# Sums over the partitions as two fp32r products of a split sum, the latents' squares added on GpSimd, and small moves on TensorE and VectorE

## The reference

```
h = concatenate([meta, x])                                # 272 x 1024
h = h + ssd_mixer(rms_norm(h, ln_mix[0]))                 # 8 groups of 256 channels, 4 heads each
h = h + square(relu(rms_norm(h, ln_mlp[0]) @ w_up)) @ w_down
h = h + mla_mixer(rms_norm(h, ln_mix[1]))                 # 16 heads, latents of 384 (q) and 256 (kv)
h = h + square(relu(rms_norm(h, ln_mlp[1]) @ w_up)) @ w_down
x = h[16:]                                                # 256 x 1024
x = x + (sigmoid(ga)*(na(q, k, v) @ w_a) + sigmoid(gb)*(cb*conv3(cc*ch) @ w_b)) @ w_o
x = x + square(relu(rms_norm(x) @ w_mlp_in)) @ w_mlp_out

# in ssd_mixer, for each of the 8 groups:
g = y * silu(z);  g = g * rsqrt(mean(g*g over the group's 256 channels) + eps)
# rms_norm: x * rsqrt(mean(x*x over the channels) + eps) * gain
```

## Time and profile before

| | |
|---|---|
| median of 3 executions | 1103.89 us (1103.84 to 1104.99) |
| profiled execution | 1103.82 us |
| its span | 1102.1 us |
| granted TensorE clock | 1.00 over the span |
| TensorE, VectorE, ScalarE, GpSimd busy | 99%, 70%, 59%, 15% |

### The profile page before, as it was taken

How to read it: one execution, slowest core, us unless ns; L and a number is a source line. 1 busy time by engine, 2 the same in 40 slices (tenths; PEclk the granted TensorE clock), 3 DMA queues, 4 the chain that set the end, 5 groups by cost and what they waited for, 6 DMA issues and landing times.

```text
span 1102.1 us, 24005 instructions
## 1 busy us (share of the span) xinstructions
PE 1094.4 (99%) x8963; PEld 1066.9 (97%) x8963; DVE 771.8 (70%) x1153; ACT 653.9 (59%) x1075; POOL 170.6 (15%) x152
## 2 busy tenths in 40 slices
PE   9999999999999999999999999999999999999998
PEld 8999999999999999988899999999999999999998
DVE  8999999778665555688676665558787687666543
ACT  7899999555554343577565554446555755554331
POOL 0445444326000000111010000000003201000000
PEclk9999999999999999999999999999999999999999
DMA  7454444575454555332265555555444555555552
GB/s 267 181 186 163 169 157 173 153 249 172 171 171 172 179 178 175 136 135 98 83 218 177 189 189 181 180 193 173 153 154 154 185 181 190 180 182 191 187 180 90
DMA packets 53226, 189.96 MB, mean 172 GB/s; under 512 B 5920, under 2 KB 7200, under 8 KB 53168
## 3 DMA queue, kind: packets, MB, share of 16 engines
q1 hardware_dynamic: 51408, 182.59, 48.4%
q0 software_dynamic: 1760, 6.59, 2.1%
HBM read 188.07 MB, written 1.08 MB: 172 GB/s over the span
## 4 chain that ended last, share of the span: by engine, by line
PE 85%; DVE 10%; ACT 2%; issue 2%; DMA 1%; POOL 0%; SPq 0%; DVEq 0%; ACTq 0%
PE lin L462 27%; PE lin L464 26%; PE lin L463 26%; DVE w_lo L1430 3%; DMA w_raw<-w 1%; PE ps L561 1%; DVE s_m L1836 1%; DVE x_lo L1440 1%; DVE p_t L1854 1%; ACT w_hi L948 0%; ACT pr L1351 0%; DVE s_m L1918 0%; PE ps L540 0%; DVE p_t L1941 0%; DVE q_ss L1779 0%
## 5 line engine op out<-in xcount | busy, mean ns | idle before, releaser
L1430 DVE TENSOR_TENSOR w_lo<-w_raw,w_hi 128x1024 fp32r<-128x1024 f32 (+3 forms) x318 | 392.6, 1237 | 237.6 <-ACT w_hi L948 236.6
L948 ACT ACTIVATE w_hi<-w_raw 128x1024 fp32r<-128x1024 f32 (+2 forms) x342 | 352.0, 1034 | 230.9 <-PE lin L464 222.0
L462 PE MATMUL lin<-x_hi,w_hi 128*128 128x256 f32 (+1 forms) x1504 | 432.1, 287 | 0.4 <-DVE x_lo L1440 0.4
L464 PE MATMUL lin<-x_hi,w_lo 128*128 128x256 f32 (+1 forms) x1504 | 428.3, 285 | 0.0
L463 PE MATMUL lin<-x_lo,w_hi 128*128 128x256 f32 (+1 forms) x1504 | 427.3, 284 | 0.0
L462 PEld LDWEIGHTS lin<-x_hi,w_hi 128*128 128x128 f32 x1504 | 283.6, 189 | 2.2 <-issue 0.8
L464 PEld LDWEIGHTS lin<-x_hi,w_lo 128*128 128x128 f32 x1504 | 283.8, 189 | 0.0
L463 PEld LDWEIGHTS lin<-x_lo,w_hi 128*128 128x128 f32 x1504 | 283.0, 188 | 0.6
L464 PE MATMUL lin<-hid_hi,w_lo 128*128 128x256 f32 (+1 forms) x768 | 218.2, 284 | 0.0
L463 PE MATMUL lin<-hid_lo,w_hi 128*128 128x256 f32 (+1 forms) x768 | 217.9, 284 | 0.0
L462 PE MATMUL lin<-hid_hi,w_hi 128*128 128x256 f32 (+1 forms) x768 | 217.4, 283 | 0.0
(11 more groups left out here) (301 smaller groups left out, 1505.5 us busy)
## 6 DMA issues: line engine op xcount, KB each, us to landing
w_raw<-w SPq DMA_DIRECT2D x342, 512.0 KB, 3.3
acs_bc<-acs_dram POOLq DMA_DIRECT2D x8, 544.0 KB, 5.9
bias_mask<-rpb POOLq DMA_DIRECT2D x4, 512.0 KB, 10.9
h<-h SPq DMA_DIRECT2D x4, 272.0 KB, 3.7
out<-h SPq DMA_DIRECT2D x8, 128.0 KB, 3.3
cst<-const SPq DMA_DIRECT2D x1, 808.0 KB, 7.1
vecs<-vec SPq DMA_DIRECT2D x1, 131.5 KB, 2.1
w_raw<-w SPq DMA_DIRECT2D x1, 128.0 KB, 4.7
```

Of the source, the lines that this page charges most:

```text
L462: mm3(o, wh, xh, start=first and i == 0, stop=False)
L464: ins = mm3(o, wl, xh, start=False, stop=last and i == kts - 1)
L948: a(w_hi[pg.slot][:, 0:n], w_raw[pg.slot][:, 0:n], ACT.Copy).then_inc(w_hi_done, pages)
L1430: tt(w_lo[pg.slot][:, 0:n], w_raw[pg.slot][:, 0:n], w_hi[pg.slot][:, 0:n].bitcast(F32), ALU.subtract)\
```

## The change

1. `group_stat`, eight times, and `norm_stat` for norms 1, 3 and 5: the fp32 product of ones with the sum becomes two fp32r products, of ones_r with the rounded sum and with the rest. GpSimd makes the rounded sum (the same addition with an fp32r output) and the rest (a subtraction that waits for both), so three operations a group in place of one, and two more a norm. ones_r is made by ScalarE in its first slot.
2. GpSimd adds kv's two tiles of squares into one and two of q's three (`add_latents`); the kv sum is three products in place of six, the q sum four in place of six.
3. `mout_part(0, ...)`: four k-tiles at t = 16 between scores(13) and p_transposes(10), in place of five at t = 17; t = 21 takes three in place of two.
4. VectorE at the start: w_lo of page 0 ahead of the last two g_lo.
5. VectorE in the second block: yb_lo from the end of i = 11 and 12 to i = 12 and 13, behind the copy of the transposed probabilities. Its operands are unchanged.

The buffers (ones_r, hs_hi, hs_lo, ys_hi, ys_lo, all fp32r) and the semaphores' declarations are left out of the diff.

```diff
@@ -485,6 +491,12 @@
             def norm_stat(norm):
                 n = width(norm)
+                if norm % 2:
+                    pe.wait_ge(hsplit_done, norm // 2 + 1)
+                    nc.tensor.matmul(ps7[:, 0:n], ones_r[:, :], hs_hi[:, 0:n], start=True, stop=False)
+                    nc.tensor.matmul(ps7[:, 0:n], ones_r[:, :], hs_lo[:, 0:n], start=False, stop=True)\
+                        .then_inc(stat_done, 1)
+                    return
                 pe.wait_ge(hsum_done, (KD - 1) * norm)
                 nc.tensor.matmul(ps7[:, 0:n], ones, h_sq[:, 0, 0:n], start=True, stop=True).then_inc(stat_done, 1)
...
@@ -545,7 +557,9 @@
             def group_stat(g):
                 pe.wait_ge(ysum_done, (g + 1).value)
                 pe.wait_ge(cbm_done, (g + 2).value) if g.base < 7 else None
-                nc.tensor.matmul(ps5[:, 0:T], ones, y_sum[:, :], start=True, stop=True).then_inc(gstat_done, 1)
+                pe.wait_ge(ones_r_done, 1)
+                nc.tensor.matmul(ps5[:, 0:T], ones_r[:, :], ys_hi[:, :], start=True, stop=False)
+                nc.tensor.matmul(ps5[:, 0:T], ones_r[:, :], ys_lo[:, :], start=False, stop=True).then_inc(gstat_done, 1)
             def y_products(g):
                 pe.wait_ge(xtok_done, (g + 1).value)
...
@@ -652,11 +666,9 @@
             lin_chunk(At(C_MIN), At(K_MIN), T, 2)
             norm_stat(2)
             lin_chunk(At(C_MIN + 1), At(K_MIN + 1), T)
-            pe.wait_ge(latsq_done, 1)
+            pe.wait_ge(latsum_done, 1)
             for b, t0 in enumerate(MLA_BLOCKS):
-                for i in range(2):
-                    ins = nc.tensor.matmul(ps5[:, b:b + 1], lat_sq[:, i, t0:t0 + P], ones[:, 0:1],
-                                           start=i == 0, stop=i == 1)
+                ins = nc.tensor.matmul(ps5[:, b:b + 1], lat_sq[:, 0, t0:t0 + P], ones[:, 0:1], start=True, stop=True)
             ins.then_inc(lstat_done, 1)
             lin_chunk(At(C_MIN + 2), At(K_MIN + 2), T)
...
@@ -666,12 +678,12 @@
             ins.then_inc(kpeT_done, 1)
             def q_stat():
-                pe.wait_ge(latsq_done, 3)
+                pe.wait_ge(latsum_done, 2)
                 pe.wait_ge(rln_done, 3)
                 for b, t0 in enumerate(MLA_BLOCKS[1:]):
-                    for i in range(3):
+                    for i in range(2):
                         ins = nc.tensor.matmul(ps7[:, b:b + 1], lat_sq[:, 3 + i, t0:t0 + P], ones[:, 0:1],
-                                               start=i == 0, stop=i == 2)
+                                               start=i == 0, stop=i == 1)
                 ins.then_inc(lstat_done, 1)
             def in_tokens(o, pg, kts, kt0, t0, n):
...
@@ -808,14 +820,14 @@
                     q_stat()
                 if 18 <= t < 21:
                     mout_part(t - 17, 5 if t < 19 else 3, 0)
-                if t == 17:
-                    mout_part(0, 5, 0)
                 if t >= 6 and t % 2:
                     p_transposes(t - 6)
                 if 1 <= t < 16 and t % 2:
                     turn_keys(t // 2)
                 if 3 <= t < 19:
                     scores(t - 3)
+                if t == 16:
+                    mout_part(0, 4, 0)
                 if t >= 6 and not t % 2:
                     p_transposes(t - 6)
                 if 2 <= t <= 16 and not t % 2:
...
@@ -823,7 +835,7 @@
                 if t in (19, 20):
                     mout_part(t - 17, 2, 3)
                 if t == 21:
-                    mout_part(0, 2, 5)
+                    mout_part(0, 3, 4)
                     mout_part(1, 2, 5)
                 if t >= 7 and t % 2:
                     values((t - 7) // 2)
...
@@ -1115,6 +1127,8 @@
                 hi((c + 3).page(0))
                 conv0(s, 1)
                 hi((c + 3).page(1))
+                act.wait_ge(const_in, 16)
+                a(ones_r[:, :], ones, ACT.Copy).then_inc(ones_r_done, 1)
                 hi((c + 4).page(0))
                 hi((c + 4).page(1))
                 for pair in range(2):
...
@@ -1475,10 +1489,10 @@
                 raw_lo(kt)
             square_raw(6)
             square_raw(7)
+            lo(Page(0), DT_PAGE)
+            dve.sem_inc(w_lo_done[1], 1)
             raw_lo(6)
             raw_lo(7)
-            lo(Page(0), DT_PAGE)
-            dve.sem_inc(w_lo_done[1], 1)
             lo(Page(2))
             dve.wait_ge(r_done, 1)
             r32 = slice(0, 32)
...
@@ -1939,6 +1953,11 @@
                     if i >= 10:
                         dve.wait_ge(pv2_done, 2 * ((i - 8) // 2))
                     nc.vector.tensor_copy(p_t2[i % 2][:, :], ps7[:, :]).then_inc(pt2_done, 1)
+                if i in (12, 13):
+                    j = i - 12
+                    dve.wait_ge(ybh_done, j + 1)
+                    tt(yb_lo[:, 2 * j:2 * j + 2, :], yb[:, 2 * j:2 * j + 2, :],
+                       yb_hi[:, 2 * j:2 * j + 2, :].bitcast(F32), ALU.subtract).then_inc(ybl_done, 1)
                 if i in (11, 12):
                     j = i - 11
                     dve.wait_ge(drained[(k + (-1)).parity], (k + (-1)).half + 1)
...
@@ -2005,13 +2024,6 @@
                             ALU.mult, ALU.add).then_inc(cv2_step, 1)
                 if 6 <= i < 14:
                     weigh2(i - 6)
-                if i in (11, 12):
-                    j = i - 11
-                    dve.wait_ge(ybh_done, j + 1)
-                    dve.wait_ge(yb_done, j + 1)
-                    tt(yb_lo[:, 2 * j:2 * j + 2, :], yb[:, 2 * j:2 * j + 2, :],
-                       yb_hi[:, 2 * j:2 * j + 2, :].bitcast(F32), ALU.subtract).then_inc(ybl_done, 1)
-
             for b in range(4):
                 c = At(C_BR + b)
...
@@ -2057,7 +2069,14 @@
                     pool.wait_ge(hsq_done, KD * norm + kt + 1)
                     if kt > 1:
                         pool.wait_ge(hsum_done, (KD - 1) * (norm - 1) + kt - 1)
+                    if norm % 2 and kt == KD - 1:
+                        tt(hs_hi[:, 0:n], h_sq[:, 0, 0:n], h_sq[:, kt, 0:n], ALU.add).then_inc(hs_hi_done, 1)
+                        pool.wait_ge(hs_hi_done, norm // 2 + 1)
                     tt(h_sq[:, 0, 0:n], h_sq[:, 0, 0:n], h_sq[:, kt, 0:n], ALU.add).then_inc(hsum_done, 1)
+                if norm % 2:
+                    pool.wait_ge(hsum_done, (KD - 1) * norm)
+                    tt(hs_lo[:, 0:n], h_sq[:, 0, 0:n], hs_hi[:, 0:n].bitcast(F32), ALU.subtract)\
+                        .then_inc(hsplit_done, 1)
             def lo(pg, n=PAGE):
...
@@ -2085,7 +2104,10 @@
                     lo((c + 2).page(1))
                 if has_stat:
                     pool.wait_ge(ysq_done, (gs + 1).value)
-                    tt(y_sum[:, :], h_sq[:, 0, :], h_sq[:, 1, :], ALU.add).then_inc(ysum_done, 1)
+                    tt(y_sum[:, :], h_sq[:, 0, :], h_sq[:, 1, :], ALU.add).then_inc(ysum_step, 1)
+                    tt(ys_hi[:, :], h_sq[:, 0, :], h_sq[:, 1, :], ALU.add).then_inc(ysum_step, 1)
+                    pool.wait_ge(ysum_step, (gs + 1).times(2).value)
+                    tt(ys_lo[:, :], y_sum[:, :], ys_hi[:, :].bitcast(F32), ALU.subtract).then_inc(ysum_done, 1)
                 if has_lin:
                     lo((c + 3).page(1))
                     if has_rows:
...
@@ -2130,6 +2152,12 @@
             for e in range(2):
                 tt(rope_q[:, :, e, :], angles[:, 1:3, :], over(cst[:, N_QGR:N_QGR + 64], 2), ALU.mult)\
                     .then_inc(rope_done, 1)
+
+            def add_latents(to, count):
+                pool.wait_ge(latsq_done, count)
+                tt(lat_sq[:, to, :], lat_sq[:, to, :], lat_sq[:, to + 1, :], ALU.add).then_inc(latsum_done, 1)
+
+            add_latents(0, 1)
             pool.wait_ge(kpe_step, 2)
             tt(kpe_sum[:, :, :], kpe_rot[:, :, 0:32], kpe_rot[:, :, 32:64], ALU.add).then_inc(kpefin_done, 1)
             pool.wait_ge(kpefin_done, 1)
...
@@ -2137,6 +2165,7 @@
             for e in range(2):
                 tt(kpe_fin[:, :, e, :], kpe_sum[:, :, :], kv_rms[:, :].unsqueeze(2).broadcast_to([P, 3, 32]), ALU.mult)\
                     .then_inc(kpefin_done, 1)
+            add_latents(4, 3)
             pool.wait_ge(kpefin_done, 3)
             pool.wait_ge(rope_done, 3)
             q_turn = rope_q[:, :, :, :].rearrange("p b h d -> p (b h) d")
```

More of the change, by code:

```diff
@@ L177, in build @@
         eps_t = sb("eps_t", [P, 4])
+        ones_r = sb("ones_r", [P, P], F32R)
+        hs_hi, hs_lo = [sb(f"hs_{n}", [P, T], F32R) for n in ("hi", "lo")]
         ssd = ExitStack()
@@ L208, in build @@
         y_sum = sb("y_sum", [P, T], F32, ssd)
+        ys_hi, ys_lo = [sb(f"ys_{n}", [P, T], F32R, ssd) for n in ("hi", "lo")]
         g_ln = sb("g_ln", [P, T], F32, ssd)
@@ L344, in build @@
         hsq_dve = sem("hsq_dve")
+        ones_r_done, hs_hi_done, hsplit_done = sem("ones_r_done"), sem("hs_hi_done"), sem("hsplit_done")
+        ysum_step = sem("ysum_step")
         rln_done, r_done = sem("rln_done"), sem("r_done")
@@ L367, in build @@
```

(1 more changed line is left out.)

## The result

The changed kernel takes 1125.34 us in the median of four executions (1124.41 to 1127.09), against 1104.15 (1103.84 to 1104.99) before: 1.019 times as long, 95% interval 1.018 to 1.021. It is slower by 21 us, where 1104.1 and no change were forecast. The profiled execution took 1124.67 us, its span is 1123.0, 20.9 more than before.

A forecast was written before the change was run, and what follows sets the result against it. TensorE, busy 99% of the span, was taken as the bound. Terms -2.2 - 0.6 + 0 + 0 + 3.1 - 0.3 + 0.8 - 0.5 = +0.3 gave 1104.1 us, 8-in-10 range 1100.5 to 1106.8.

The forecast's parts named there:

- The group sums' product: State-space part: two fp32r products in place of one fp32 product on TensorE save 0.20 us a group, eight 1.6.
- the norms: Three MLP norms: the same replacement of the fp32 product saves 0.2 + 2 x 0.19 = 0.58 us.
- the kv latents: Latents' squares: six of twelve one-column records on TensorE go, 0.105 each, -0.63 us.
- The queries' sum: Four records go, but TensorE's transposes wait for q_n, whose chain does not move: 0 taken, bound -0.42 us.
- the price of the turns in the steady slots: GpSimd's added operations each wait for one VectorE operation; ys_lo is ready before TensorE's 115.63: 0, bound +3.0 us.
- Rival (c): Steady slots: VectorE is the bound and a page comes late, up to 0.5 us a slot, 1107.1; chance 0.13.
- The tail: End of the state-space part: TensorE waits for ys_lo, +2.4 at group 6, +0.7 at group 7; +3.1 us, range +1.2 to +4.1.
- The start: TensorE's 0.33 idle at the dt products goes as w_lo comes earlier: -0.3 us, range 0 to -0.5.
- The projection's first tile: Near 524, moved products fill TensorE's waits but values(5) comes 0.45 later: +0.8 us, other bound -1.2.
- yb_lo: TensorE's 0.66 wait at 833.79 for a copy behind this operation shrinks: -0.5 us, range -0.2 to -0.65.

The follow-up runs named there:

- experiment 4: Changed kernel with the third x_tok (16 partitions) moved on VectorE from ahead of the first mm to between the two mm: 1106.48 us (1.0018).
- e5_no_start: Changed kernel with the group sums' change undone and the order at the start as before too: 1102.72 us (0.9987 of the kernel before).
- the first probe: VectorE and GpSimd alone, none of the reference computed; GpSimd released at 22 moments around a run of VectorE operations on 128 partitions: nothing over 1.66 us.
- the second, with a narrow operation ahead: VectorE and GpSimd alone, the slot's piece around ys_lo at 12 moments: with 16 partitions in the third x_tok 4.5 to 4.7 us at some, with 128 always 0.76.

## Why the prediction was wrong

- **The group sums' product, the norms, the kv latents** were right: a slot of 22.00 against 22.20; -0.21 at norm 1; -0.68 for -0.63. The queries' sum, forecast at 0 with a bound of -0.42, gave -0.3: the attention part takes 101.90 with it alone and 102.21 before.
- **The step that failed** is the price of the turns in the steady slots, GpSimd held off by "its neighbour's" length: "ys_hi follows until about 113.4, ys_lo until 114.3, at worst (each behind an operation of 0.9) 115.4". The worst case had each GpSimd operation behind one of VectorE's, as in every row of before. ys_lo was kept out by four. In the steady slots I took 0, bound +3.0, and it was +18.8: 3.2 us at the first sum and 2.7 at each of five more (24.69 for 22.00), with 3.1 of slower clock behind two of them, less 1.0 that the products save. Nothing of before shows such a case, because there no GpSimd operation starts between the narrow x_tok and the run; the bound was made from rows that had met only the easy case. What could be read in the same trace is the run itself, which the prediction did not lay beside its own times. Of VectorE, before:

```profile
113.67 2.01 DVE L1571 TENSOR_TENSOR mm<-ee,cbm 128x864 f32<-128x864 f32 x2
115.61 0.71 DVE L1547 TENSOR_TENSOR xs_s<-cv,sg 128x544 f32<-128x544 f32 x1
116.24 1.21 DVE L1430 TENSOR_TENSOR w_lo<-w_raw,w_hi 128x1024 fp32r<-128x1024 f32 x1
```

With ys_hi until 113.4, ys_lo would start some 0.3 ahead of this run, and a bound by the whole of it is 3.8.
- **Rival (c)** had the right sign for the wrong reason: VectorE was busy for a smaller share of the slots, and TensorE waited in them for ys_lo and for no page.
- **The tail** was mis-sized by phase: +1.1 net of what the products save there, for a forecast of +2.5 so counted (3.1 less three times 0.2). In the changed kernel everything comes at other moments there, group 6 does not wait, and group 7 waits 1.43. In the kernel of experiment 4, where the tail is reached as before, it costs +2.4, close to the forecast's. The range's lower end of 1.2 held group 6 alone; with the 0.65 of group 7 it is 1.8.
- **The start**: -0.3 forecast, range 0 to -0.5; +2.15 in the profiled execution. In the medians it is about +0.9 (1103.62 against 1102.72), from intervals that overlap. The sum took TensorE's row alone and had no term for the clamp and w_lo meeting. The explanation in the expectation of e5_no_start, that the earlier w_lo gets ahead of the clamp, does not hold: the clamp starts first, and at the same distance both outcomes are on record. Held clamps were seen with the new order only, in four of seven traces against none of six with the old; whether the order brings them is open.
- **The projection's first tile**: +0.8 forecast, +0.74 by the traces with and without it. **yb_lo**: -0.5 forecast; the wait at 833.79 is gone, and the second block with norm 5 is 0.72 shorter, 0.53 without the norm.

The terms that failed, the steady slots, the tail and the start, are all about GpSimd and VectorE meeting; the others were within 0.3. The Trainium skill ("SBUF — State Buffer", SBUF: two separate sides) says that whichever of the two starts first gets the shared pair of ports for its instruction. In the first probe, all on 128 partitions, the runs agree, down to 0.02 us. In the second, with a narrow operation ahead, they do not: ys_lo starts 0.20 ahead of mm and takes 4.59 for 0.76. Nor do they at the start, where the clamp begins 0.29 ahead of w_lo and is held for 2.5.

What stays open: why an operation on fewer than 128 partitions does this, how long its effect lasts (two operations of 128 partitions behind it don't end it, and whether the convolution's do was not tried), whether the distance to the run or the narrow operation's start sets its edge, what decides between clamp and w_lo, and what picks the waits behind which the clock falls.

## What to carry to other kernels

Before an operation is put on GpSimd, look at which run of VectorE operations with SBUF operands its start falls ahead of: the bound for it is the length of the whole run, not of one operation, above all where an operation on fewer than 128 partitions stands ahead, and the order of small operations on VectorE can decide between the two. A gain in a loop is worth only what the first wait behind the loop leaves of it. Where two engines share something, price their meeting both ways, and take more than one trace: the same meeting can end either way.

## What the runs showed that I had not expected

- With an operation of 16 to 96 partitions on VectorE ahead in the same stretch, a GpSimd operation that starts between 0.33 us ahead of a run of VectorE's two-operand SBUF work and 0.03 inside it is kept out of the whole run (4.36 to 4.73 in the probes instead of 0.76). From 0.10 inside it waits for one operation alone. With 128 partitions only, it goes first even when it starts 0.02 ahead, and inside an operation it waits for that one.
- A VectorE clamp with one SBUF operand can be held off too by a GpSimd subtraction, even one that starts 0.29 behind it: 3.04 instead of 0.55, in four of eleven such meetings.
- Behind a wait of TensorE of 2.46, within 1.4 us of its end, the granted clock fell to 0.50 for 3.4 us in some slots (products at 0.227 instead of 0.126), 1.6 us each time, and in others, with waits of the same length, it did not.
